# Up by token halves: a first pass over 256 tokens, then one pass that does up and down for the other 256

## What is computed

```
s = jnp.einsum("thpd,hpkd->thpk", q, sub_keys)
top_v, top_i = lax.top_k(s, PEER_TOPK)
comb = top_v[:, :, 0, :, None] + top_v[:, :, 1, None, :]   # 16 x 16 sums
best_v, best_j = lax.top_k(comb, PEER_TOPK)
idx = i1 * N_KEYS + i2
gate = jax.nn.softmax(best_v, axis=-1)
a = jnp.einsum("tmd,td->tm", u_tab[ib], xb)
wgt = gb * jax.nn.gelu(a)
y = jnp.einsum("tm,tmd->td", wgt, v_tab[ib])
```

## Time and profile before

| | us |
|---|---|
| median of 3 runs | 3184.18 |
| lowest, highest | 3183.21, 3186.78 |
| the profiled execution, whole | 3189.15 |
| its span in the trace | 3187.3 |
| PE busy | 3091.1 (97%) |
| DVE busy | 2457.8 (77%) |
| POOL busy | 1185.7 (37%) |
| ACT busy | 1118.5 (35%) |
| DMA | 734.76 MB, 231 GB/s over the span |

### The profile page before, as it was taken

The page is one execution under the profiler, slowest core; times in us unless marked ns, Lnnn a source line. Parts: engine busy times, 40 slices in busy tenths (PEclk is TensorE's granted clock), DMA queues, the critical chain, the costliest instruction groups (busy, mean ns, idle before and its releaser), DMA issues.

```text
span 3187.3 us, 54768 instructions
## 1 busy us (share of the span) xinstructions
PE 3091.1 (97%) x16200; PEld 2682.7 (84%) x16200; DVE 2457.8 (77%) x5952; ACT 1118.5 (35%) x1590; POOL 1185.7 (37%) x765
## 2 busy tenths in 40 slices
PE   6989999999999999999999999999999999999998
PEld 4668888778888899999975788888788889999997
DVE  7981999859995488999977239951799926889987
ACT  3333322234443333333343332223344433333333
POOL 0033445420001366766700334544000024667674
PEclk8999999999999999999999999999999999999999
DMA  6162666445556799999921224444455578999996
GB/s 254 62 216 101 241 231 240 165 139 188 215 207 256 254 362 361 360 361 363 374 91 40 85 82 142 147 145 141 149 218 210 189 287 293 362 358 361 361 371 238
DMA packets 278481, 734.76 MB, mean 231 GB/s; under 512 B 36064, under 2 KB 118368, under 8 KB 276448
## 3 DMA queue, kind: packets, MB, share of 16 engines
q1 hardware_dynamic: 186688, 462.03, 41.7%
q0 software_dynamic: 50688, 151.18, 12.8%
q10 hardware_dynamic: 40992, 120.34, 9.6%
HBM read 613.85 MB, written 119.54 MB: 230 GB/s over the span
## 4 chain that ended last, share of the span: by engine, by line
PE 54%; POOL 18%; issue 14%; DVE 10%; DMA 2%; ACTq 1%; ACT 1%; DVEq 0%; SPq 0%; POOLq 0%
PE bank L507 30%; PE bank L511 15%; POOL z_pad L934 9%; POOL u_pad L928 5%; PE bank L616 3%; POOL z_pad L928 2%; POOL scratch L928 2%; PE bank L528 2%; DVE scratch L1285 2%; PE bank L427 1%; ACTq L826 1%; DVE h L1266 1%; DVE h L1263 1%; PE bank L451 1%; DVE h L1265 1%
## 5 line engine op out<-in xcount | busy, mean ns | idle before, releaser
L507 PE MATMUL bank<-h_hi,w_hi 128*128 128x512 f32 x2528 | 997.9, 395 | 19.2 <-ACT norm_tmp L807 16.3
L673 ACT ACTIVATE w_hi<-ring 128x1024 fp32r<-128x1024 f32 x584 | 615.0, 1053 | 1116.0 <-PE bank L511 1036.8
L507 PE MATMUL bank<-h_lo,w_hi 128*128 128x512 f32 x2528 | 988.2, 391 | 0.0
L913 POOL TENSOR_TENSOR w_lo<-ring,w_hi 128x1024 fp32r<-128x1024 f32 x172 | 442.8, 2575 | 844.2 <-ACT w_hi L673 844.1
L633 PE MATMUL bank<-v_lo,w_hi 128*128 128x368 f32 x2032 | 670.5, 330 | 0.0
L633 PE MATMUL bank<-v_hi,w_hi 128*128 128x368 f32 x2032 | 665.2, 327 | 2.7 <-DVE v_lo L1439 1.8
L511 PE MATMUL bank<-h_hi,w_lo 128*128 128x512 f32 x2528 | 624.3, 389 | 0.0
L507 PEld LDWEIGHTS bank<-h_hi,w_hi 128*128 128x128 f32 x2528 | 476.9, 189 | 119.4 <-ACT w_hi L673 19.1
L507 PEld LDWEIGHTS bank<-h_lo,w_hi 128*128 128x128 f32 x2528 | 476.7, 189 | 97.1
L511 PEld LDWEIGHTS bank<-h_hi,w_lo 128*128 128x128 f32 x2528 | 474.5, 188 | 98.6
L934 POOL DMA_INDIRECT z_pad<-ga_scratch,z_pad x288 | 374.0, 1299 | 155.0 <-issue 86.9
(11 more groups left out here) (184 smaller groups left out, 2885.0 us busy)
## 6 DMA issues: line engine op xcount, KB each, us to landing
ring<-u_t SPq DMA_DIRECT2D x256, 512.0 KB
ring<-v_t SPq DMA_DIRECT2D x256, 512.0 KB
ga_scratch<-norm_tmp ACTq DMA_DIRECT2D x256, 256.0 KB, 2.0
g_scratch<-scratch ACTq DMA_DIRECT2D x12, 4096.0 KB, 13.8
scratch<-ga_scratch SPq DMA_DIRECT2D x256, 192.0 KB
scratch<-ada_t SPq DMA_DIRECT2D x76, 512.0 KB, 5.8
scratch<-g_scratch SPq DMA_DIRECT2D x32, 768.0 KB
keys<-g_scratch SPq DMA_DIRECT2D x32, 768.0 KB
```

The lines of the kernel that those rows point to most:

```text
L507: pe.matmul(to, w_hi[:, b, k * P:(k + 1) * P], part_h[:, k, :], start=(k == 0 and part_h is h_hi), stop=False)
L673: return act.activation(to, of, ACT.Copy)
L913: pool.tensor_tensor(w_lo[:, n % 2, :], ring[:, n % RING, :], w_hi[:, n % 2, :].bitcast(F32), ALU.subtract).then_inc(tile_used[n % RING], 1)
```

## The change

The 512 tokens are cut in two halves: `DENSE` = the first 256, `SPARSE` = the last 256.

- First pass: `up_chunk` computes the up product for the 256 sparse tokens only (128x256 matmuls), beside retrieval and gates. GELU values of these tokens are stored (128 KB a chunk).
- Fused pass: the `u_t` tiles are loaded again. For each chunk PE does the up product of the dense tokens and, two chunks behind, the down product of the same tokens (48 matmuls of 128x256). GELU values of the dense tokens stay on the chip, in `norm_tmp`. The eight output blocks of 256 tokens lie in four PSUM banks, and the two banks 6 and 7 take the up results.
- The sparse tokens: 256 rows of `v_t` and 256 cells are fetched by POOL in each layer (144 before), and added by DVE, two in each chunk of the fused pass. 16 buffers hold rows, cells run 12 ahead.
- Gates are scattered for 256 tokens, 32 chunks (48 before). The one-hot rows of 8 tokens are made by four float16 instructions of 1024 elements instead of 24 of 128.
- The scores are computed within wq, key set by key set, and the 16-best search over key sets starts there. 100 candidate sums a head (3 rows of 16, 13 of 4) replace 256. The index search is in float16, with one comparison and one product of 4096 elements and a tree of additions.
- Eight modulation tiles of layer 0 move from wq to the retrieval (56 in place of 48 there). `RETRIEVING` is 72 chunks (56 before), and the modulation tiles come three in each round of four chunks, from round 1.

```diff
-    RETRIEVING = 14 * N_U // 32
+    RETRIEVING = 18 * N_U // 32
+    DENSE = T // 2
+    SPARSE = T - DENSE
+    TURNS = SPARSE // P * PICKS
+    ROWS = 16
...
+    FIRST_ADDS = (0, 0, 2, 2, 3, 3, 3, 3)
+    CELLS_AHEAD = 12
...
-                    product(l, r, stages["u"] + s, bank[:, s % 2, :])
+                    product(l, r, stages["u"] + s, bank[:, s % 2, 0:SPARSE], slice(DENSE, T))
...
+                def fused_up(q, i, n):
+
+                    pe.wait_ge(act_done, N_U * l + STEP * q + (i + 1))
+                    product(l, RING * q, n, bank[:, 6 + i % 2, 0:DENSE], slice(0, DENSE))
...
+                with pe.Fori(1, BLOCKS) as q:
+                    for i in range(STEP):
+                        fused_up(q, i, F + 2 * i - 2)
+                        down(q, i, F + 2 * i - 1)
...
+                for n in range(ROWS):
                     pool.wait_ge(split_hi, CHUNKS * l + (stages["u"] + EARLY + LATE + n + 1))
+                    fetch_row(n)
                 for s in range(RING):
                     pool.wait_ge(ga_stored[s], 16 * (N_U // RING) * l + 16 * (N_U // RING) + 16)
...
+                for n in range(CELLS_AHEAD):
+                    fetch_cell(n)
+                for n in range(ROWS, TURNS):
+                    fetch_cell(n - ROWS + CELLS_AHEAD)
+                    pool.wait_ge(rows_used, TURNS * l + n + 1)
+                    fetch_row(n)
...
+                    link(dve.tensor_tensor(eq_4, ranks.unsqueeze(2).to_broadcast(shape4),
+                                           iota_rank.unsqueeze(1).to_broadcast(shape4), ALU.is_equal))
+                    link(dve.tensor_tensor(eq_4, eq_4, idx_h.unsqueeze(3).to_broadcast(shape4), ALU.mult))
...
+                        dve.tensor_tensor(hot1[:, b, 1, :, :, :], table, along(i1_t), ALU.is_equal).then_inc(hot_step, 1)
+                        dve.tensor_tensor(hot2[:, b, :, :], iota_b[:, :].unsqueeze(1).to_broadcast([P, TOK, P]),
+                                          i2_t[:, cols].unsqueeze(2).to_broadcast([P, TOK, P]), ALU.is_equal)
+                        dve.wait_ge(hot_step, LATE * l + RING * r + s + 1)
+                        dve.tensor_tensor(hot1[:, b, 0, :, :, :], hot1[:, b, 1, :, :, :], along(ghi_t), ALU.mult)
+                        dve.tensor_tensor(hot1[:, b, 1, :, :, :], hot1[:, b, 1, :, :, :], along(glo_t), ALU.mult)\
...
+                def fused(q, i, turns, to):
+
+                    turns = list(turns)
+                    low(q, F + 2 * i)
+                    weights(q, i)
+                    for m in turns[:len(turns) // 2]:
+                        add(q, m, to)
+                    low(q, F + 2 * i + 1)
+                    low_weights(q, i)
+                    for m in turns[len(turns) // 2:]:
+                        add(q, m, to)
```

740 lines of the change are left out of this document (355 added, 385 removed).

## The result

The changed kernel takes 3415.31 us (median of 4 runs, 3395.34 to 3418.39) beside 3185.48 us before (4 runs). The ratio is 1.0708, with a 95% interval of 1.0666 to 1.0750. The forecast was 3144 us in a range of 3050 to 3275: wrong in sign and outside the range.

What follows compares the result with a forecast made beforehand. POOL's DMA instructions were to bound the fused pass, four engines lying within 8%. Layer 0 was 301+23+131+52+789 = 1296 us (+22), layer 1 1219 (-61), together -39 or -40: 3144 us, range 3050 to 3275.

Steps and rivals of the forecast that it cites:

- PE: Everywhere: a 256-column matmul costs 120 ns, so 5.75 us a fused chunk; PE's work is 1134 us a layer, 1256 before.
- First pass, exclusion of DVE and POOL: First pass: DVE and POOL low parts take turns on the port; retrieval takes 301 us in layer 0, 224 in layer 1.
- the other step named there: Layer 0's first pass: SP's modulation loads wait for DVE ahead of `u_t` tiles, spreading the delay but adding nothing.
- float16: Retrieval and gates: between half and full float32 price, 9.5 us a tile's 4096-element chain, 0.7 us a gate instruction.
- The sum of 4.1 us a chunk: Gates: DVE's low part and four float16 instructions, with waits, take 4.1 us a chunk, 131 us for 32.
- Rival 4: Retrieval and gates: float16 costs the float32 price, gates 5.75 us a chunk, launch 3282 us; 0.33 for all slower rivals together.
- Last 16 chunks: Last 16 chunks before the fused pass: 46 us on PE, 62 us by DMA traffic, taken as 52 us.
- Fused pass, 789 us a layer: Fused pass: POOL sets the end, 496 DMA instructions at 1.58 us make 784 us, plus 5 us for the last add.
- rival 3: Fused pass: DVE's long instructions stretch POOL's to 1.80 us, launch 3362 us; no gain from 1.62; 0.33 for all slower rivals.
- DMA, 767 us by 361 GB/s: Fused pass: DMA engines need 767 us for 277 MB a layer at 361 GB/s.
- DVE's adds waiting for rows: Fused pass sign: with PE below 95% busy and POOL's gaps 0.30 us throughout, it would confirm the forecast's reading.
- POOL instructions of 1.5 us and more: rival 3: Fused pass sign: POOL instructions this long would show that rival 3 holds.

Runs made afterwards that it cites:

- no_adds: Changed kernel with DVE's sparse-token adds cut from 1024 to 32 elements, fetches and waits as before: 3366.38 us, 1.0561 times the kernel before.
- no_cells: Changed kernel without POOL's 512 cell fetches and DVE's waits for them; rows, adds and tiles stay: 3110.46 us, 0.9758 times the kernel before.
- burst: Changed kernel without cells for weights, adds of 32 elements, plus 32 unused cell fetches before rows 64, 128 and 192: 3213.09 us, 1.0085 times the kernel before.
- lead6: Changed kernel with at most 6 rows fetched and not yet added (16 before), cells 20 ahead; same work: 3333.93 us, 1.0459 times the kernel before.

## Why the prediction was wrong, step by step

- **PE: right.** 120 ns a matmul of 256 columns, measured 119 to 120, and 5.76 us a fused chunk.
- **First pass, exclusion of DVE and POOL: right.** Layer 0's retrieval ends at 629.73, 307 us after the scores (forecast 301), PE is at 74% there and at 93% in layer 1, and 33 of 79 low parts take over 3 us. In layer 1 DVE was done after 202 us (224), and the gates still began after 256 us (247), because 72 chunks took 229 us and not 207: POOL's low parts reach 2.4 us and more of 2.87. Rows of layer 0 show both engines taking turns: a cast of 128 elements and a small subtraction last as long as POOL's low part beside them.

```profile
590.34 2.52 POOL L950 TENSOR_TENSOR w_lo<-ring,w_hi 128x1024 fp32r<-128x1024 f32 x1 [0.42 <-ACT w_hi L700]
...
590.63 2.31 DVE L1348 CAST u_pad<-u_pad 128x128 f16<-128x128 f32 x1
...
593.22 2.45 POOL L950 TENSOR_TENSOR w_lo<-ring,w_hi 128x1024 fp32r<-128x1024 f32 x1 [0.36 <-ACT w_hi L700]
593.44 2.38 DVE L1351 TENSOR_TENSOR u_pad<-u_pad 128x128 f16<-128x128 f32 x1
...
598.18 4.42 DVE L1354 TENSOR_TENSOR z_pad<-z_pad,u_pad 128x4096 f16<-128x4096 f16 x1
...
604.34 0.34 SPq L335 DMA_DIRECT2D scratch<-ada_t  x1
...
609.40 1.06 ACT L700 ACTIVATE w_hi<-ring 128x1024 fp32r<-128x1024 f32 x1 [15.98 <-DMA ring<-u_t]
```

  The last two rows are the other step named there: SP's modulation load at 604.34 had waited for DVE, the `u_t` tiles behind it with it, and ACT stood 15.98 us.
- **float16.** The index search has two instructions of 4096 elements. One (L1352) is 2.29 us, the other (L1354) 4.42 us at the least. In the gates three of the four instructions of 1024 elements are 0.68 us long and one, `hot2` at L1422, 1.22 us. The Trainium skill's table (VectorE: DVE Perf Modes, "The perf-mode tier table") halves `tensor_tensor` on 16-bit data; that holds for three of four here, not for L1422. For this speed the same page of the Trainium skill ("Mode 2×_1P — pack two bf16 into one 32-bit read") asks for 16-bit elements that lie one step apart. L1422 and L1354 are the two with an operand that repeats one value along the innermost axis, so the trace agrees; the prediction used the table without this condition. The sum of 4.1 us a chunk was right all the same: the 32 low parts lie from 660.12 to 787.74. Rival 4 didn't come.
- **Last 16 chunks: 56 and 57 us from the first high part of the stage to the first of the fused pass, forecast 52.** ACT waits 6.2 and 7.9 us for a `u_t` tile at the end, with the DMA engines full (389 GB/s): the 62 us of traffic that the forecast set aside in part.
- **Fused pass, 789 us a layer: this step failed.** It was the sum of one engine, POOL, at one price: "I take 1.28 + 0.30 = 1.58 us", the mean of the earlier trace rows with the gap of the earlier trace rows. That mean belonged to a DVE with other work: before, a down chunk had one low part and one add or two. In the fused pass DVE is busy 65.17 of 66 us with long instructions while PE runs freely, and POOL's DMA instruction costs 1.83 us there, each 2.67 us in the worst stretch. This was rival 3, at 1.80 us: 898 us a pass. Measured were 910 and 894. It had stood in the text as the strongest objection, with a break-even of 1.62 us, and was given too small a chance. The same mechanism had been priced rightly for POOL's low parts earlier in the text, and then a mean from a kinder neighbourhood was used for its DMAs. Yet the price is only part of it, and that rival 3's number fits is partly luck. POOL itself took 1.75 and 1.73 us an instruction, waited 73 us of the first pass for free buffers, and was done 31 us before the end, so it wasn't the plain bound that both the forecast and rival 3 made of it; and with the price brought down to some 1.4 us (no_adds) the passes still took 883 and 872 us. What the sum left out is that PE and ACT, which it let run freely beside POOL, are held up: 175 us of PE's time in the first pass.
- **DMA, 767 us by 361 GB/s: wrong too**, without harm. no_cells carries 389 GB/s, by which the 277 MB take 712 us. A DMA share of 0.99 at 359 GB/s in the earlier trace rows was read as a ceiling.
- **The range.** It was said to take in rival 4, but that stood at 3282 us and the range ended at 3275. Measured were 3415, above every rival, rival 3's 3362 included.
- **What the profile was to show.** "DVE's adds waiting for rows": not seen. "POOL instructions of 1.5 us and more: rival 3": seen only in stretches, 121 of 496 in each pass; the mean of 1.31 us hides it, because POOL is quick whenever DVE stands.

**What stays open.** The cause of most of the loss. First, with both kinds of fetch the long adds are not needed: no_adds stays at 3366 us, though its POOL could issue four instructions in 5.7 us, while rows alone or cells alone at that rate are at PE's bound. Second, why PE halts inside a product and ACT starts late with all inputs there. It happens in every kernel with four DMA instructions a chunk and long adds, in no_adds with short ones, and without tile traffic; it is not seen in burst, nor with short adds and one kind of fetch. Late supply of instructions to PE and ACT was not tried. The trace gives it no support: in the stretch from 959 to 997 us, in which PE halts, the DMA engines have packets of the two data queues q0 and q1 alone and none of the instruction queues q8 and q14.

No version with all of the work beat the kernel before; the best was lead6, at 1.046 times its time.

## What to carry to other kernels

Price an instruction on a shared port by the neighbour that it will have, not by its mean in the old kernel: take the rows in which that neighbour runs without a gap. Count DMA instructions of GpSimd for each step of a pipeline like matmuls, and give them slack; here three a chunk were nearly free, and four beside long adds cost 115 to 165 us a pass, at any number of bytes. A cheap instruction alone is no promise: no_adds had one, and lost nearly as much. When several engines come to within 8% of each other, a stall isn't made up: POOL's catching up, ACT's late starts and PE's lower clock (0.59 in the stretch shown) follow one another, and a smaller lead (6 rows for 16) was the better one here.
